# Moving an FFT convolution's spectral product from VectorE to GpSimd, and attention's weights-times-values product to split fp32r form

## The chip, the cores and the metric

The kernel runs on one core of a Trainium2 chip. The metric is the device time of one execution in microseconds. The kernel before takes 966.35 us, the median of three runs (965.32 to 966.81).

## What is computed

One layer of a bidirectional encoder on 512 tokens of width 1024, in float32: half a SwiGLU step, a mixing stage, another half SwiGLU step, a final norm. The change lies in the mixing stage, whose two groups of heads share one input projection:

```python
p = h @ w_in                                   # q | k | v | hyena x0 | x1 | v
logits = einsum('bqhcd,bkhcd->bhcqk', q, k) * scale + bias
attn   = softmax(logits)[c=0] - lam * softmax(logits)[c=1]     # 4 heads, two maps each
out    = einsum('bhqk,bkhe->bqhe', attn, v)                    # weights times values
...
v = v * x1                                     # hyena, after a width-3 convolution
y = irfft(rfft(v, n=2L) * rfft(kern, n=2L))[:L]                # long convolution
y = (y + v * filt_bias) * x0
```

## The kernel before, in words

Everything is laid out as 128 partitions by 512 tokens. TensorE (PE) does every large product in fp32r, a form that takes one pass but keeps fewer bits; so that nothing is lost, each operand x is held as x_hi, an fp32r copy made by ScalarE (ACT), and x_lo = x - x_hi, made by VectorE (DVE), and a product is three passes, hi·hi, hi·lo and lo·hi. A plain float32 product takes one instruction, which the trace records twice.

The mixing stage is a program written out by hand for each engine; semaphores keep the engines apart, and the order on each engine is fixed. PE runs 24 `project(n)` tiles (24 matmuls each: 8 blocks k by 3 passes), and between them the attention of head h = 0 to 3:

- `two_scores(h, qb)`: query times key for two query blocks, into banks 2 to 5. It waits for `qk_split` (DVE's `split_qk`, the low parts of q and k).
- DVE `logits(h, qb)` adds the bias (bank and bias, 128x512, twice); ACT `exps(h, qb)` takes exponentials and their sums; DVE `combine(h, qb)` forms one block of `attn` in three instructions: a reciprocal, a small `scalar_tensor_tensor` on two columns of `stat` (L1788), and a wide one on the two halves of `prob` (L1791).
- PE `attend_turns(h)` waits for all four blocks (`attn_set`) and transposes key blocks kt = 0 and 1 of `attn` into banks 4 and 5 (L2557, four transposes a block); ACT `attn_turns` copies each to `attn_t` (L1006). It stands behind k = 6 of `project(13)`, `project(17)` or `project(21)`.
- PE `attend(h)` multiplies `v_nat` by `attn_t` for four key blocks (L2576), in plain float32 for heads 0 to 2, with the turns of kt = 2 and 3 between the products, since there are two banks. Head 3 (`last_attend`) has the split form: `v_hi`, `v_lo`, `attn_hi` and `attn_low`.

DVE has more to do between these: `project(n)` reads a finished tile from its bank (times `rinv`), `split(8, n)` makes the low part of the next weights from `raw` and `w_hi` (L1227), `taps(n)` does two steps of the short convolution on `zpad` and `x0c` (L1746, L1747), and the spectral product of the long convolution is spread in pairs of instructions over heads 0 to 2: `cross_near`, `cross_far`, `own_near`, `own_far`, `imaginary`, `real`, `real_parities`, `imaginary_parities`, for the two halves f = 0 and 1 of the frequencies, 16 instructions each. The half f can begin when DVE's `cosines(f)` and `sines(f)` are done (`spec_read`). PE's `inverse(g)`, in head 3, waits for `spec_set` 2, the end of the last pair.

GpSimd (POOL) has in this stage only the four DMA issues of `bias`, one a head. Elsewhere it adds squares for the norms (L585) with a 128x512 `tensor_tensor`.

Of the kernel before, what the change touches and what calls it, by code (L numbers as in the profile page):

```python
# [14 lines left out]
P = 128  # L15
D = 1024
S = 512
# [86 lines left out]
def build(nc, a, out):  # L104
    ctx = ExitStack()
    with ctx:
# [74 lines left out]
        def h_high(ffn, f):  # L181
# [41 lines left out]
        v_nat, _ = place("v_nat", [P, NT, P], at=act3_at)  # L223
        v_hi, _ = place("v_hi", [P, NT, P], F32R, at=act3_at)
        v_lo, _ = place("v_lo", [P, NT, P], F32R, at=bias_at)
        attn_hi, _ = place("attn_hi", [P, NT, S], F32R, at=attn_t_at)
        attn_lows = [place(f"attn_lo{n}", [P, S], F32R, at=at + 4 * 3 * S)[0] for n, at in enumerate((x0c_at, vx_at))]
# [92 lines left out]
        dft_even, dft_sum, spec_even, evens_set, spec_read, spec_set, kern_evens = (  # L320
            sem(n) for n in ("dft_even", "dft_sum", "spec_even", "evens_set", "spec_read", "spec_set", "kern_evens"))
# [242 lines left out]
        def _(pool):  # L564
# [47 lines left out]
            for h in range(HEADS):  # L612
                wait(pool, logit_set, 2 * NT * (h - 1))
                toeplitz = bass.AP(vec_dram.tensor, vec_dram.offset + h * 2 * S, [[1, P], [1, bias_w]])
                pool.dma_start(bias[:, h % 2, :], toeplitz).then_inc(bias_landed[h % 2], 16)

# [12 lines left out]
        def _(act):  # L629
# [368 lines left out]
            def v_natural(h):  # L998
                act.wait_ge(v_turned, h + 1)
                nc.scalar.copy((v_hi if h == 3 else v_nat)[:], bank[TURN_BANKS[h]][:].rearrange("p (t c) -> p t c", t=NT)).then_inc(v_set, 1)  # L1000

            def attn_turns(h, kts):
                wait(act, att_col_sum, h)
                for kt in kts:
                    act.wait_ge(attn_turned, NT * h + kt + 1)
                    nc.scalar.copy((attn_hi if h == 3 else attn_t)[:, kt, :], bank[4 + kt % 2][:]).then_inc(attn_t_set, 1)  # L1006
# [100 lines left out]
            attn_turns(1, (0, 1))  # L1107
            split(8, N_MIX + 19)
            qk_high(2, 1)
            attn_turns(1, (2, 3))  # L1110
# [12 lines left out]
            attn_turns(2, (0, 1))  # L1123
            split(8, N_MIX + 23)
            qk_high(3, 1)
            attn_turns(2, (2, 3))
# [87 lines left out]
        def _(dve):  # L1214
# [542 lines left out]
            def v_low():  # L1757
                dve.wait_ge(v_set, HEADS)
                nc.vector.tensor_tensor(v_lo[:], bank[TURN_BANKS[3]][:].rearrange("p (t c) -> p t c", t=NT),
                                        v_hi[:].bitcast(F32), ALU.subtract).then_inc(v_split, 1)  # L1760

            def attn_low(kt):

                dve.wait_ge(attn_turned, NT * 3 + kt + 1)
                dve.wait_ge(attn_t_set, NT * 3 + kt + 1)
                nc.vector.tensor_tensor(attn_lows[kt % 2][:], bank[4 + kt % 2][:], attn_hi[:, kt, :].bitcast(F32),
                                        ALU.subtract).then_inc(attn_split, 1)
# [29 lines left out]
            def kernel_parities(c):  # L1797

                dve.wait_ge(kern_even, c + 1)
                even, twice = bank[4][:], ksig[:, 2 * c + 1, :]  # L1800
                nc.vector.tensor_tensor(ksig[:, 2 * c, :], even, twice, ALU.add)
                x, y = (twice, even) if c else (even, twice)
                nc.vector.tensor_tensor(twice, x, y, ALU.subtract).then_inc(kern_evens, 1)
                dve.wait_ge(kern_evens, c + 1)
# [13 lines left out]

            def mult(dst, x, y):
                return nc.vector.tensor_tensor(dst, x, y, ALU.mult)  # L1820

            t0, t1, t2, t3 = (prod[:, i, :] for i in range(4))
# [22 lines left out]
            def sines(f):  # L1845
# [6 lines left out]
                dve.wait_ge(spec_read, f + 1)  # L1852

            def cross_near(f):
                near_a, far_a, near_b, far_b = parts(f)
                dve.wait_ge(kern_set, 4)
                mult(t0, near_a, kern_q[:, f, :])
                link(mult(t1, near_b, kern_p[:, f, :]))

            def cross_far(f):  # L1860
                near_a, far_a, near_b, far_b = parts(f)
                mult(t2, far_a, kern_q[:, 2 + f, :])
                link(mult(t3, far_b, kern_p[:, 2 + f, :]))

            def own_near(f):
                near_a, far_a, near_b, far_b = parts(f)
                mult(near_a, near_a, kern_p[:, f, :])
                link(mult(near_b, near_b, kern_q[:, f, :]))

            def own_far(f):  # L1870
                near_a, far_a, near_b, far_b = parts(f)
                mult(far_a, far_a, kern_p[:, 2 + f, :])
                link(mult(far_b, far_b, kern_q[:, 2 + f, :]))

            def imaginary(f):

                nc.vector.tensor_tensor(t0, t0, t1, ALU.add)
                link(nc.vector.tensor_tensor(t2, t2, t3, ALU.add))

            def real(f):  # L1880

                near_a, far_a, near_b, far_b = parts(f)
                nc.vector.tensor_tensor(kern_p[:, f, :], near_a, near_b, ALU.subtract)
                link(nc.vector.tensor_tensor(kern_p[:, 2 + f, :], far_a, far_b, ALU.subtract))

            def real_parities(f):

                near, far = kern_p[:, f, :], kern_p[:, 2 + f, :]
                nc.vector.tensor_tensor(kern_q[:, f, :], near, far, ALU.add)
                link(nc.vector.tensor_tensor(kern_q[:, 2 + f, :], near, far, ALU.subtract))  # L1890

            def imaginary_parities(f):

                nc.vector.tensor_tensor(kern_p[:, f, :], t0, t2, ALU.subtract)
                nc.vector.tensor_tensor(kern_p[:, 2 + f, :], t0, t2, ALU.add).then_inc(spec_set, 1)
                dve.wait_ge(spec_set, f + 1)
# [106 lines left out]
            cross_near(0)  # L2003
# [12 lines left out]
            own_far(0)  # L2016
            combine(1, 0)
            logits(1, 1)
            imaginary(0)
            project(14)  # L2020
            combine(1, 1)
            real(0)
            split(8, N_MIX + 16)
            real_parities(0)
# [8 lines left out]
            imaginary_parities(0)  # L2033
            project(16)
            split(8, N_MIX + 18)
            cross_near(1)
            project(17)
            split_qk(2, 0)
            split_qk(2, 1)
            cross_far(1)  # L2040
# [3 lines left out]
            own_near(1)  # L2044
            combine(2, 0)
            logits(2, 1)
            own_far(1)
            project(18)
            combine(2, 1)
            imaginary(1)  # L2050
            split(8, N_MIX + 20)
            real(1)
# [8 lines left out]
            real_parities(1)  # L2061
            project(20)
            split(8, N_MIX + 22)
            imaginary_parities(1)
            project(21)
            split_qk(3, 0)
# [34 lines left out]
            v_low()  # L2101
            attn_low(0)
            attn_low(1)
            split(8, N_OUT + 1)
            attn_low(2)
            attn_low(3)
# [69 lines left out]
        def _(pe):  # L2176
# [294 lines left out]
            def two_scores(h, qb):  # L2471

                if qb == 0:
                    pe.wait_ge(logit_set, 2 * NT * h)
                    pe.wait_ge(attn_t_set, NT * h)
# [49 lines left out]
            def turn_v(h):  # L2525
# [3 lines left out]
                wait(pe, v_set, h)  # L2529
# [22 lines left out]
            def turn(h, kt):  # L2552
                if h == 3:
                    wait(pe, attn_split, kt - 1)
                wait(pe, attn_t_set, NT * h + kt - 1)
                for qb in range(NT):
                    ins = nc.tensor.transpose(bank[4 + kt % 2][:, qb * P:(qb + 1) * P],  # L2557
# [3 lines left out]
            def attend_turns(h):  # L2561
# [4 lines left out]
                turn(h, 0)  # L2566
                turn(h, 1)

            def attend(h):
# [9 lines left out]
                ins.then_inc(pv_sum, 1)  # L2579

            def last_attend():
                pe.wait_ge(att_o_set, 3)
                pe.wait_ge(v_split, 1)
                for kt in range(NT):
                    pe.wait_ge(attn_t_set, NT * 3 + kt + 1)
                    nc.tensor.matmul(bank[6][:], v_hi[:, kt, :], attn_hi[:, kt, :], start=kt == 0, stop=False)
                    nc.tensor.matmul(bank[6][:], v_lo[:, kt, :], attn_hi[:, kt, :], start=False, stop=False)
                    pe.wait_ge(attn_split, kt + 1)
                    ins = nc.tensor.matmul(bank[6][:], v_hi[:, kt, :], attn_lows[kt % 2][:], start=False, stop=kt == NT - 1)
                    if kt + 2 < NT:  # L2590
                        turn(3, kt + 2)
                ins.then_inc(pv_sum, 1)

            def att_sums(h):
# [4 lines left out]
                else:  # L2599
                    pe.wait_ge(v_set, 3)  # L2600
# [83 lines left out]
            def out_half(n, jj):  # L2684
# [3 lines left out]
                if part and jj == 0:  # L2688
                    if pair == 1:
                        pe.wait_ge(hy_scaled, NG)  # L2690
                    elif pair == 2:
                        pe.wait_ge(attn_split, NT)
# [75 lines left out]
            project(13, between={6: lambda: attend_turns(0)})  # L2768
# [9 lines left out]
            project(17, between={6: lambda: attend_turns(1)})  # L2778
# [9 lines left out]
            project(21, between={6: lambda: attend_turns(2)})  # L2788
# [16 lines left out]
            last_attend()  # L2805
# [116 lines left out]
```

## Time and profile before

| | |
|---|---|
| median of three runs | 966.35 us |
| the profiled execution, device time | 966.17 us |
| its span in the profile | 964.4 us |
| PE busy | 958.1 us (99%) |
| PE weight loads busy | 826.7 us (86%) |
| DVE busy | 693.2 us (72%) |
| ACT busy | 439.9 us (46%) |
| POOL busy | 87.9 us (9%) |

The span is what the profiler saw from the first to the last instruction; the device time has 1.8 us around it. Matmuls overlap in their pipeline, and the end that the profile shows for one is modelled: the pace of PE is read from start to start, not from durations. A start of a DVE instruction that waits for a port lies before the wait, so the wait shows as a longer instruction.

### The profile page before, as it was taken

How to read it: one execution, taken by the hardware profiler on the slowest of the kernel's cores; microseconds unless marked ns; L12 is line 12 of the kernel's file. 1: busy time of each engine (PE TensorE's matmuls, PEld its weight loads, DVE VectorE, ACT ScalarE, POOL GpSimd, SP SyncE). 2: the span in 40 equal slices, each digit the busy share in tenths (PEclk: the TensorE clock that was granted, in tenths of full speed). 3: DMA queues.
4: the chain of work that ended last, by engine and by line, in shares of the span. 5: the costliest groups of instructions: out<-in, count | busy, mean ns of one | idle time of the engine just before them, and what ended most of it. 6: DMA issues, size and time to landing. Idle time of an engine off the chain costs nothing.

```text
span 964.4 us, 15111 instructions
## 1 busy us (share of the span) xinstructions
PE 958.1 (99%) x5487; PEld 826.7 (86%) x5487; DVE 693.2 (72%) x1072; ACT 439.9 (46%) x699; POOL 87.9 (9%) x104
## 2 busy tenths in 40 slices
PE   9999999999999999999999999999999999999998
PEld 8889999999888887677777878889999999988887
DVE  6888897887754438868898775789897788742333
ACT  6345665546333233244455563446565554622222
POOL 0011121210011010000000000001112121000100
PEclk9999999999999999999999999999999999999999
DMA  7456768674433336121221332256777767333322
GB/s 228 142 142 174 197 169 196 169 192 141 138 99 101 99 125 240 66 81 51 84 86 45 113 117 88 92 149 155 187 193 171 203 162 191 102 104 99 90 69 88
DMA packets 55029, 128.67 MB, mean 133 GB/s; under 512 B 5954, under 2 KB 14287, under 8 KB 54724
## 3 DMA queue, kind: packets, MB, share of 16 engines
q1 hardware_dynamic: 44452, 107.31, 34.7%
q0 software_dynamic: 10384, 20.67, 12.3%
q8 instruction: 30, 0.49, 0.2%
q14 instruction: 19, 0.16, 0.1%
q10 hardware_dynamic: 144, 0.05, 0.1%
HBM read 123.78 MB, written 4.22 MB: 133 GB/s over the span
## 4 chain that ended last, share of the span: by engine, by line
PE 94%; DVE 3%; issue 1%; ACT 1%; DVEq 0%; POOL 0%; ACTq 0%; POOLq 0%
PE bank L2185 14%; PE bank L2187 14%; PE bank L2186 14%; PE bank L2243 8%; PE bank L2242 8%; PE bank L2241 8%; PE bank L2233 7%; PE bank L2235 3%; PE bank L2705 1%; PE bank L2707 1%; PE bank L2706 1%; PE bank L2576 1%; PE bank L2328 1%; PE bank L2329 1%; PE bank L2330 1%
## 5 line engine op out<-in xcount | busy, mean ns | idle before, releaser
L1227 DVE TENSOR_TENSOR w_lo<-raw,w_hi 128x1024 fp32r<-128x1024 f32 (+1 forms) x94 | 113.2, 1204 | 105.9 <-ACT w_hi L638 105.6
L638 ACT CAST w_hi<-raw 128x1024 fp32r<-128x1024 f32 (+1 forms) x94 | 95.0, 1011 | 187.4 <-PE bank L2187 172.4
L2185 PE MATMUL bank<-x_hi,w_hi 128*128 128x512 f32 x320 | 128.3, 401 | 0.1
L2186 PE MATMUL bank<-h_lo,w_hi 128*128 128x512 f32 x330 | 128.4, 389 | 0.0
L2187 PE MATMUL bank<-x_hi,w_lo 128*128 128x512 f32 x320 | 124.7, 390 | 0.0
L2186 PE MATMUL bank<-x_lo,w_hi 128*128 128x512 f32 x320 | 124.7, 390 | 0.0
L2241 PE MATMUL bank<-xt_both,w_hi 128*128 128x256 f32 x408 | 115.6, 283 | 0.0
L2243 PE MATMUL bank<-xt_both,w_lo 128*128 128x256 f32 x408 | 115.5, 283 | 0.0
L2242 PE MATMUL bank<-xt_both,w_hi 128*128 128x256 f32 x408 | 115.4, 283 | 0.0
L2241 PEld LDWEIGHTS bank<-xt_both,w_hi 128*128 128x128 f32 x408 | 77.6, 190 | 0.1
L2243 PEld LDWEIGHTS bank<-xt_both,w_lo 128*128 128x128 f32 x408 | 77.6, 190 | 0.0
L2242 PEld LDWEIGHTS bank<-xt_both,w_hi 128*128 128x128 f32 x408 | 77.6, 190 | 0.0
L2242 PE MATMUL bank<-xt_both,wt_hi 128*128 128x256 f32 x272 | 77.0, 283 | 0.0
L2243 PE MATMUL bank<-xt_both,wt_lo 128*128 128x256 f32 x272 | 77.0, 283 | 0.0
L2241 PE MATMUL bank<-xt_both,wt_hi 128*128 128x256 f32 x272 | 76.7, 282 | 0.0
L2185 PEld LDWEIGHTS bank<-x_hi,w_hi 128*128 128x128 f32 x320 | 60.1, 188 | 17.2 <-issue 5.6
L2186 PEld LDWEIGHTS bank<-h_lo,w_hi 128*128 128x128 f32 x330 | 61.9, 188 | 12.8
L2187 PEld LDWEIGHTS bank<-x_hi,w_lo 128*128 128x128 f32 x320 | 60.1, 188 | 12.8
L2186 PEld LDWEIGHTS bank<-x_lo,w_hi 128*128 128x128 f32 x320 | 60.2, 188 | 12.3 <-issue 0.7
L2185 PE MATMUL bank<-h_hi_t,w_hi 128*128 128x512 f32 x180 | 70.0, 389 | 0.0
L2187 PE MATMUL bank<-h_hi_t,w_lo 128*128 128x512 f32 x180 | 70.0, 389 | 0.0
L1494 DVE TENSOR_TENSOR wt_lo<-raw,wt_hi 128x1024 fp32r<-128x1024 f32 x34 | 41.6, 1224 | 29.7 <-ACT wt_hi L758 29.5
(392 smaller groups left out, 2142.6 us busy)
## 6 DMA issues: line engine op xcount, KB each, us to landing
raw<-in_ffn_w_down SPq DMA_DIRECT2D x32, 512.0 KB, 3.6
raw<-in_ffn_w_gate SPq DMA_DIRECT2D x25, 512.0 KB, 4.0
raw<-in_ffn_w_up SPq DMA_DIRECT2D x25, 512.0 KB, 4.6
raw<-in_w_in SPq DMA_DIRECT2D x24, 512.0 KB, 3.3
raw<-in_ffn_w_gate SPq DMA_DIRECT2D x34, 256.0 KB, 3.1
raw<-in_ffn_w_up SPq DMA_DIRECT2D x34, 256.0 KB, 3.1
raw<-in_ffn_w_down SPq DMA_DIRECT2D x16, 384.0 KB, 3.1
sums<-in_ffn_w_gate SPq DMA_DIRECT2D x17, 256.0 KB, 3.7
```

The lines of the kernel that those rows point to most:

```text
L638: nc.scalar.copy(w_hi[:, half, 0:kb, :], raw[:, slot, 0:kb, :]).then_inc(w_hi_made, 1)
L1227: nc.vector.tensor_tensor(w_lo[:, half, 0:kb, :], raw[:, slot, 0:kb, :], w_hi[:, half, 0:kb, :].bitcast(F32), ALU.subtract).then_inc(w_spl ...
L1494: nc.vector.tensor_tensor(wt_lo[:, 0:2].rearrange("p t k c -> p (t k) c"), raw[:, 2 * b, :, :], hi.bitcast(F32), ALU.subtract).then_inc(pa ...
L2185: nc.tensor.matmul(dst, w_hi[:, half, k, :], hi, start=first and k == 0, stop=False)
L2186: nc.tensor.matmul(dst, w_hi[:, half, k, :], lo, start=False, stop=False)
L2187: ins = nc.tensor.matmul(dst, w_lo[:, half, k, :], hi, start=False, stop=last and k == kb - 1)
L2233: nc.tensor.matmul(bank[n][:], high[:, k, :], xt_both[ffn][:, m, k].rearrange("p t c -> p (t c)"), start=start and k == 0, stop=False, ski ...
L2235: ins = nc.tensor.matmul(second_half(n), low[:, k, :], xt_hi[ffn][:, m, k, :], start=False, stop=k == 3, skip_group_check=True)
L2241: nc.tensor.matmul(dst, high[:, k, :], xt_hi[ffn][:, m, k, :], start=start and k == 0, stop=False, skip_group_check=True)
L2242: nc.tensor.matmul(dst, high[:, k, :], xt_lo[ffn][:, m, k, :], start=False, stop=False, skip_group_check=True)
L2243: ins = nc.tensor.matmul(dst, low[:, k, :], xt_hi[ffn][:, m, k, :], start=False, stop=which == 3 and k == 3, skip_group_check=True)
L2328: nc.tensor.matmul(dst, hi[:, k, :], h_ops[1][f][0][:, tokens], start=f == 0, stop=False)
```

## The change

The spectral product leaves DVE. POOL does it in `spectrum(f)`, pair by pair, with a wait for its own semaphore behind each pair; the bias transfers of heads 2 and 3 are issued behind `spectrum(0)` and `spectrum(1)`. Attention's product takes the split form in all heads: `v_low` and `attn_low` on DVE for each head, three passes on PE for each key block. For heads 0 to 2 all four key blocks are turned at once, into banks 4, 5, 2 and 3, behind k = 5 of the project tile instead of k = 6. ACT copies the four blocks in a row; `qk_high(h+1, 1)` moves ahead of a weight split.

```diff
+            def two(dsts, xs, ys, ops):
+                made[0] += 1
+                nc.gpsimd.tensor_tensor(dsts[0], xs[0], ys[0], ops[0])
+                nc.gpsimd.tensor_tensor(dsts[1], xs[1], ys[1], ops[1]).then_inc(spec_made, 1)
+                pool.wait_ge(spec_made, made[0])
+
+            def spectrum(f):
+                near_a, near_b, far_a, far_b = ((sig0, sig1)[f][:, i, :] for i in range(4))
+                t0, t1, t2, t3 = (prod[:, i, :] for i in range(4))
+                p_near, p_far, q_near, q_far = (kern[:, i, :] for kern in (kern_p, kern_q) for i in (f, 2 + f))
+                pool.wait_ge(kern_set, 4)
+                pool.wait_ge(spec_read, f + 1)
+                two((t0, t1), (near_a, near_b), (q_near, p_near), (ALU.mult, ALU.mult))
+                two((t2, t3), (far_a, far_b), (q_far, p_far), (ALU.mult, ALU.mult))
+                two((near_a, near_b), (near_a, near_b), (p_near, q_near), (ALU.mult, ALU.mult))
+                two((far_a, far_b), (far_a, far_b), (p_far, q_far), (ALU.mult, ALU.mult))
+                two((t0, t2), (t0, t2), (t1, t3), (ALU.add, ALU.add))
+                two((p_near, p_far), (near_a, far_a), (near_b, far_b), (ALU.subtract, ALU.subtract))
+                two((q_near, q_far), (p_near, p_near), (p_far, p_far), (ALU.add, ALU.subtract))
+                nc.gpsimd.tensor_tensor(p_near, t0, t2, ALU.subtract)
+                nc.gpsimd.tensor_tensor(p_far, t0, t2, ALU.add).then_inc(spec_set, 1)
+                pool.wait_ge(spec_set, f + 1)
+
+            head_bias(0)
+            head_bias(1)
+            spectrum(0)
+            head_bias(2)
+            spectrum(1)
+            head_bias(3)
...
             qk_high(1, 0)
-            attn_turns(0, (0, 1))
+            attn_turns(0, range(NT))
+            qk_high(1, 1)
             split(8, N_MIX + 15)
-            qk_high(1, 1)
-            attn_turns(0, (2, 3))
             attended(0)
...
             combine(0, 2)
-            cross_near(0)
             logits(0, 3)
             project(12)
             combine(0, 3)
-            cross_far(0)
+            v_low(0)
             split(8, N_MIX + 14)
+            split_qk(1, 0)
+            attn_low(0, 0)
+            attn_low(0, 1)
+            attn_low(0, 2)
             project(13)
-            split_qk(1, 0)
+            attn_low(0, 3)
             split_qk(1, 1)
-            own_near(0)
             split(8, N_MIX + 15)
 
             logits(1, 0)
-            own_far(0)
             combine(1, 0)
...
-                turn(h, 0)
-                turn(h, 1)
+                for kt in range(2 if h == 3 else NT):
+                    turn(h, kt)
 
             def attend(h):
                 wait(pe, att_o_set, h)
                 if h in (1, 2):
                     pe.wait_ge(att_mean, h)
-                pe.wait_ge(v_set, h + 1)
+                pe.wait_ge(v_split, h + 1)
                 for kt in range(NT):
                     pe.wait_ge(attn_t_set, NT * h + kt + 1)
-                    ins = nc.tensor.matmul(bank[6][:], v_nat[:, kt, :], attn_t[:, kt, :], start=kt == 0, stop=kt == NT - 1)
-                    if kt + 2 < NT:
+                    nc.tensor.matmul(bank[6][:], v_hi[:, kt, :], attn_hi[:, kt, :], start=kt == 0, stop=False)
+                    nc.tensor.matmul(bank[6][:], v_low_part(h)[:, kt, :], attn_hi[:, kt, :], start=False, stop=False)
+                    pe.wait_ge(attn_split, NT * h + kt + 1)
+                    ins = nc.tensor.matmul(bank[6][:], v_hi[:, kt, :], attn_low_part(h, kt)[:], start=False, stop=kt == NT - 1)
+                    if h == 3 and kt + 2 < NT:
                         turn(h, kt + 2)
...
-            project(13, between={6: lambda: attend_turns(0)})
+            project(13, between={5: lambda: attend_turns(0)})
```

DVE's order changes in heads 1 and 2 as in head 0. `two_scores(h+1, 0)` waits for `attn_split` instead of `attn_t_set`, since DVE now reads the turned banks too. The low parts lie in parts of `vx` and `x0c` that are free by then.

## Rows read from the trace of the kernel before

**Rows 1.** The page: TensorE's granted clock by slice, and the chain that ended last.
```profile
PEclk9999999999999999999999999999999999999999
...
PE 94%; DVE 3%; issue 1%; ACT 1%; DVEq 0%; POOL 0%; ACTq 0%; POOLq 0%
```

**Rows 2.** PE's timeline, head 2: start, length, instruction, how many in a row.
```profile
502.08 0.39 PE L2185 MATMUL bank<-x_hi,w_hi 128*128 128x512 f32 x1
...
507.98 0.39 PE L2187 MATMUL bank<-x_hi,w_lo 128*128 128x512 f32 x1
508.30 0.50 PE L2486 MATMUL bank<-k_hi,q_hi 64*128 64x512 f32 x2
...
525.88 1.02 PE L2576 MATMUL bank<-attn_t,v_nat 128*128 128x512 f32 x2
526.73 0.60 PE L2557 MATMUL bank<-ident,attn 128*128 128x128 f32 x4
527.17 1.02 PE L2576 MATMUL bank<-attn_t,v_nat 128*128 128x512 f32 x2
528.03 0.60 PE L2557 MATMUL bank<-ident,attn 128*128 128x128 f32 x4
528.74 1.98 PE L2576 MATMUL bank<-attn_t,v_nat 128*128 128x512 f32 x4
530.65 0.50 PE L2486 MATMUL bank<-k_hi,q_hi 64*128 64x512 f32 x2
```

**Rows 3.** PE's timeline, head 0: block k = 6, the turns, the first product, the next scores.
```profile
459.22 0.39 PE L2185 MATMUL bank<-x_hi,w_hi 128*128 128x512 f32 x1
...
459.90 1.03 PE L2557 MATMUL bank<-ident,attn 128*128 128x128 f32 x8
...
461.47 1.02 PE L2576 MATMUL bank<-attn_t,v_nat 128*128 128x512 f32 x2
...
465.96 0.51 PE L2486 MATMUL bank<-k_hi,q_hi 64*128 64x512 f32 x2
```

**Rows 4.** The groups of instructions: copies of turned blocks, and low parts from a bank.
```profile
L1006 ACT COPY attn_t<-bank 128x512 f32<-128x512 f32 x12 | 6.7, 585 | 1.9 <-PE bank L2557 1.9
L1766 DVE TENSOR_TENSOR attn_lo<-bank,attn_hi 128x512 fp32r<-128x512 f32 x4 | 2.7, 685 | 1.0 <-ACT attn_hi L1006 1.0
```

**Rows 5.** One line, POOL's 128x512 additions: shortest, median and longest in ns.
```profile
L585 POOL TENSOR_TENSOR ssq<-ssq,sq x15: 1287/1294/1717, 255.6 to 941.8; 128x512 f32<-128x512 f32 x15
```

**Rows 6.** Timelines of POOL and DVE where an addition on POOL meets a DVE instruction.
```profile
342.28 1.30 POOL L585 TENSOR_TENSOR ssq<-ssq,sq 128x512 f32<-128x512 f32 x1 [13.67 <-ACT sq L646]
...
342.70 1.43 DVE L1282 SCALAR_TENSOR_TENSOR x_lo<-resid,cols,x_hi 128x512 fp32r<-128x512 f32 x1 [1.31 <-ACT x_hi L651]
...
357.13 0.75 DVE L1282 SCALAR_TENSOR_TENSOR x_lo<-resid,cols,x_hi 128x512 fp32r<-128x512 f32 x1 [0.79 <-ACT x_hi L651]
358.07 1.23 DVE L1227 TENSOR_TENSOR w_lo<-raw,w_hi 128x1024 fp32r<-128x1024 f32 x1 [0.19 <-ACT w_hi L638]
...
358.73 1.72 POOL L585 TENSOR_TENSOR ssq<-ssq,sq 128x512 f32<-128x512 f32 x1 [15.15 <-ACT sq L646]
...
911.78 1.29 POOL L585 TENSOR_TENSOR ssq<-ssq,sq 128x512 f32<-128x512 f32 x1 [13.68 <-ACT sq L646]
...
912.59 1.56 DVE L1227 TENSOR_TENSOR w_lo<-raw,w_hi 128x1024 fp32r<-128x1024 f32 x1 [1.11 <-ACT w_hi L638]
```

**Rows 7.** DVE's timeline from the first half's sines to head 0's last combine.
```profile
441.77 0.68 DVE L1851 TENSOR_TENSOR sig<-sig,bank 128x512 f32<-128x512 f32 x1
...
447.48 0.22 DVE L1788 SCALAR_TENSOR_TENSOR stat<-stat,lam 128x1 f32<-128x1 f32 x1
...
453.38 0.75 DVE L1791 SCALAR_TENSOR_TENSOR attn<-prob,stat 128x512 f32<-128x512 f32 x1
...
458.11 0.75 DVE L1791 SCALAR_TENSOR_TENSOR attn<-prob,stat 128x512 f32<-128x512 f32 x1
```

**Rows 8.** PE's timeline: the first matmul of the inverse transform, in head 3.
```profile
537.82 0.60 PE L2639 MATMUL bank<-sin_i,kern_p 128*128 128x128 f32 x4
```

More of the change, by code:

```diff
@@ L222, in build, with v_low_part, attn_low_part, turned_bank @@
         assert top[0] <= tail_end
[L223 removed]
         v_hi, _ = place("v_hi", [P, NT, P], F32R, at=act3_at)
[L225 removed]
+        v_lows = [place(f"v_lo{n}", [P, NT, P], F32R, at=at)[0] for n, at in enumerate((vx_at + 4 * S, bias_at))]
         attn_hi, _ = place("attn_hi", [P, NT, S], F32R, at=attn_t_at)
[L227 removed]
+        attn_lows = [place(f"attn_lo{n}", [P, S], F32R, at=at)[0]
+                     for n, at in enumerate((vx_at, vx_at + 4 * 3 * S, vx_at + 4 * 2 * S, x0c_at + 4 * 3 * S))]
+        def v_low_part(h):
+            return v_lows[h == 3]
+        def attn_low_part(h, kt):
+            return attn_lows[kt] if h < 3 else attn_lows[1 if kt % 2 else 3]
+        def turned_bank(h, kt):
+            return bank[4 + kt % 2] if h == 3 or kt < 2 else bank[kt]
         q_lo, _ = place("q_lo", [P, S], F32R, at=q_t_at)
@@ L611, in _, with head_bias @@
             nc.gpsimd.memset(zpad[:], 0.0).then_inc(consts_set, 1)
-            for h in range(HEADS):
+            def head_bias(h):
                 wait(pool, logit_set, 2 * NT * (h - 1))
@@ L999, in v_natural @@
                 act.wait_ge(v_turned, h + 1)
-                nc.scalar.copy((v_hi if h == 3 else v_nat)[:], bank[TURN_BANKS[h]][:].rearrange("p (t c) -> p t c", t=NT)).then_inc(v_set, 1)
+                nc.scalar.copy(v_hi[:], bank[TURN_BANKS[h]][:].rearrange("p (t c) -> p t c", t=NT)).then_inc(v_set, 1)
             def attn_turns(h, kts):
@@ L1005, in attn_turns @@
                     act.wait_ge(attn_turned, NT * h + kt + 1)
-                    nc.scalar.copy((attn_hi if h == 3 else attn_t)[:, kt, :], bank[4 + kt % 2][:]).then_inc(attn_t_set, 1)
+                    nc.scalar.copy(attn_hi[:, kt, :], turned_bank(h, kt)[:]).then_inc(attn_t_set, 1)
             def attended(h):
@@ L1106, in _ @@
             qk_high(2, 0)
-            attn_turns(1, (0, 1))
+            attn_turns(1, range(NT))
+            qk_high(2, 1)
             split(8, N_MIX + 19)
-            qk_high(2, 1)
-            attn_turns(1, (2, 3))
             attended(1)
@@ L1122, in _ @@
             qk_high(3, 0)
-            attn_turns(2, (0, 1))
+            attn_turns(2, range(NT))
+            qk_high(3, 1)
             split(8, N_MIX + 23)
-            qk_high(3, 1)
-            attn_turns(2, (2, 3))
             attended(2)
@@ L1755, in taps, with v_low, attn_low @@
                     nc.vector.tensor_tensor(far, count(1 + S, -1), count(1, 1), ALU.subtract).then_inc(vx_set, 1)
-            def v_low():
-                dve.wait_ge(v_set, HEADS)
-                nc.vector.tensor_tensor(v_lo[:], bank[TURN_BANKS[3]][:].rearrange("p (t c) -> p t c", t=NT),
+            def v_low(h):
+                dve.wait_ge(v_set, h + 1)
+                nc.vector.tensor_tensor(v_low_part(h)[:], bank[TURN_BANKS[h]][:].rearrange("p (t c) -> p t c", t=NT),
                                         v_hi[:].bitcast(F32), ALU.subtract).then_inc(v_split, 1)
[L1762 to L1766, printed above, removed]
+            def attn_low(h, kt):
+                dve.wait_ge(attn_turned, NT * h + kt + 1)
+                dve.wait_ge(attn_t_set, NT * h + kt + 1)
+                nc.vector.tensor_tensor(attn_low_part(h, kt)[:], turned_bank(h, kt)[:], attn_hi[:, kt, :].bitcast(F32),
                                         ALU.subtract).then_inc(attn_split, 1)
@@ L1802, in kernel_parities @@
                 x, y = (twice, even) if c else (even, twice)
-                nc.vector.tensor_tensor(twice, x, y, ALU.subtract).then_inc(kern_evens, 1)
-                dve.wait_ge(kern_evens, c + 1)
+                link(nc.vector.tensor_tensor(twice, x, y, ALU.subtract))
             def kernel_spectrum(k):
@@ L1851, in sines @@
                 nc.vector.tensor_tensor(near_b, near_b, sin_odd, ALU.add).then_inc(spec_read, 1)
[L1852 to L1896, printed above, removed]
             def long_read_out(g):
@@ L2032, in _ @@
             att_means(0)
-            imaginary_parities(0)
+            v_low(1)
             project(16)
             split(8, N_MIX + 18)
-            cross_near(1)
+            split_qk(2, 0)
+            attn_low(1, 0)
+            attn_low(1, 1)
+            attn_low(1, 2)
             project(17)
-            split_qk(2, 0)
+            attn_low(1, 3)
             split_qk(2, 1)
-            cross_far(1)
             split(8, N_MIX + 19)
             logits(2, 0)
-            own_near(1)
             combine(2, 0)
             logits(2, 1)
-            own_far(1)
             project(18)
             combine(2, 1)
-            imaginary(1)
             split(8, N_MIX + 20)
-            real(1)
             logits(2, 2)
@@ L2060, in _ @@
             att_means(1)
-            real_parities(1)
+            v_low(2)
             project(20)
             split(8, N_MIX + 22)
-            imaginary_parities(1)
+            split_qk(3, 0)
+            attn_low(2, 0)
+            attn_low(2, 1)
+            attn_low(2, 2)
             project(21)
-            split_qk(3, 0)
+            attn_low(2, 3)
             split_qk(3, 1)
@@ L2100, in _ @@
             hy_low(3)
-            v_low()
-            attn_low(0)
-            attn_low(1)
+            v_low(3)
+            attn_low(3, 0)
+            attn_low(3, 1)
             split(8, N_OUT + 1)
-            attn_low(2)
-            attn_low(3)
+            attn_low(3, 2)
+            attn_low(3, 3)
             split(8, N_OUT + 2)
@@ L2474, in two_scores @@
                     pe.wait_ge(logit_set, 2 * NT * h)
-                    pe.wait_ge(attn_t_set, NT * h)
+                    wait(pe, attn_split, NT * h)
                 for q in (qb, qb + 1):
@@ L2528, in turn_v @@
                 pe.wait_ge(spec_read, 2)
-                wait(pe, v_set, h)
+                wait(pe, v_split, h)
                 if h == 3:
@@ L2552, in turn @@
             def turn(h, kt):
-                if h == 3:
-                    wait(pe, attn_split, kt - 1)
-                wait(pe, attn_t_set, NT * h + kt - 1)
+                wait(pe, attn_split, NT * h + (kt - 1 if h == 3 else 0))
                 for qb in range(NT):
-                    ins = nc.tensor.transpose(bank[4 + kt % 2][:, qb * P:(qb + 1) * P],
+                    ins = nc.tensor.transpose(turned_bank(h, kt)[:, qb * P:(qb + 1) * P],
                                               attn[:, qb, kt * P:(kt + 1) * P], ident[:])
@@ L2599, in att_sums @@
                 else:
-                    pe.wait_ge(v_set, 3)
+                    pe.wait_ge(v_split, 3)
                 if h == 2:
@@ L2691, in out_half @@
                     elif pair == 2:
-                        pe.wait_ge(attn_split, NT)
+                        pe.wait_ge(attn_split, NT * HEADS)
                     elif pair == 3:
@@ L2777, in _ @@
             project(16)
-            project(17, between={6: lambda: attend_turns(1)})
+            project(17, between={5: lambda: attend_turns(1)})
             attend(1)
@@ L2787, in _ @@
             project(20)
-            project(21, between={6: lambda: attend_turns(2)})
+            project(21, between={5: lambda: attend_turns(2)})
             attend(2)
@@ L2804, in _ @@
             first_out({0: lambda: spread(3)})
-            last_attend()
+            attend(3)
             out_tile(1)
```

23 lines of the change are left out of this document (3 added, 20 removed).

## The prediction

> **What bounds the kernel now.** I began with the page: the chain that ended last is 94% PE, and the granted clock is full, 2.4 GHz, in every slice [rows 1]. So time is what PE's stream contains, plus any moment at which it waits. The profiled execution took 966.17 us (span 964.4, 1.77 around it); the median is 966.35, so the sum below may start from either. Next I read PE's timeline where the change is, start to start [rows 2, 3], then DVE's just ahead of head 0's turns [rows 7], because DVE sets when PE may turn, and last the few places where POOL computes beside DVE [rows 5, 6].
>
> **PE's own saving.** An fp32r pass takes (507.98 - 502.08)/26 = 0.227 us; the step from such a pass into the scores is 0.32, 0.1 more [rows 2]. A plain product takes 0.85 (525.88 to 526.73), four transposes 0.44 (526.73 to 527.17), and there is a wait of 528.74 - 528.03 - 0.44 = 0.27 for ACT's copy [rows 2]. Head 2's attend lasts 525.88 to 530.65, 4.77, of which 0.88 is turns: 3.89. Head 1 repeats it within 0.02. Head 0's is 4.49 (461.47 to 465.96), 3.61 without turns [rows 3]. The new one is 12 passes of 0.227 and the step of 0.1, 2.82. Saved: 0.79 + 1.08 + 1.07 = 2.94 us. The turns only move: sixteen transposes a head, as before, so nothing. If no new wait comes, that is 966.17 - 2.94 = 963.2.
>
> **What the new product waits for.** After four turns (1.75) come k = 6 and 7 (1.36), then the first pass, 3.1 us behind the first turn. Four copies of 0.585 on ACT and four `attn_low` of 0.685 on DVE [rows 4], the latter back to back, keep up with 0.68 us a key block if DVE is there when the first copy is, about 1.2 us behind the first turn. Ahead of them DVE has `v_low` (0.6), a weight split (1.2) and `split_qk` (0.6): 2.4. So DVE must end `combine(h, 3)` some two us ahead of the time at which PE would like to turn. The semaphore changes (`v_split` for `v_set`, `attn_split` for `attn_t_set`) cost nothing: the last pass of `attend` has already waited for them.
>
> **DVE's relief.** 32 spectral instructions go, 15 low parts come, each about 0.6 at its pace. In head 0 two of them stood ahead of `logits(0, 3)`, so its last combine, over at 458.86 [rows 7], would be over near 457.5. PE reaches the turns, now ahead of k = 6, at 459.22 [rows 3]: 1.7 us of slack.
>
> **POOL's price.** A 128x512 addition takes 1.29 us on POOL [rows 5]; multiply and subtract have no row and are taken as the same, with zero to 2.6 each as bounds. 32 of them are 41 us. POOL starts when the first sines are done, 441.77 + 0.69 = 442.5 [rows 7], and fills heads 0 and 1. Its own deadline is far: even stretched by half it ends near 505, and `inverse` starts at 537.82 [rows 8]. The bias of head 2 goes out near 469, a head (32 us, half of 465.96 to 530.65) ahead of its use. Alone, POOL costs nothing.
>
> But it isn't alone. When `x_lo` began at 342.70, inside POOL's addition of 342.28 to 343.58, it took 1.43 instead of 0.75, ending 0.55 behind the addition; `w_lo` at 912.59, inside 911.78 to 913.07, took 1.56 instead of 1.23; and the addition that began at 358.73 inside `w_lo` took 1.72 instead of 1.29 [rows 6]. All eleven meetings in the trace look so: whoever is second stands still until the first is done. In each the DVE instruction reads two operands from SBUF. The Trainium skill (SBUF — State Buffer, Who interferes with whom) makes it a rule: the two engines share a port pair, locked for a whole instruction, and a VectorE instruction with at most one SBUF input doesn't take it. By that rule logits, bank reads and low parts stay free; no row shows one under an addition. I count them as free, the nearest rows having two SBUF inputs; if they too are held, head 0 gains eight more meetings of up to 1.29 each.
>
> **Head 0, worked through.** Between 442.5 and the last combine DVE has nine instructions with two SBUF inputs: three combines of two (L1788, L1791), a split, two taps. I let additions run back to back (0.1 between pairs), let a waiting DVE instruction in when one ends, and give it 0.55 from there (1.1 for a split). `combine(0, 1)`: the small one waits from 447.48 to addition 4's end, 447.8; the wide one comes behind addition 5 and ends 449.75. The split waits for addition 7 and ends 453.6. The taps end 455.45 and 457.3, behind 8 and 9. `combine(0, 2)` waits for 10 and for 11 and ends 460.6 (before 454.13 [rows 7]). Logits, a read and ACT's exponentials take until 463.0; the last combine, behind additions 13 and 14, ends at 465.3. PE wanted it at 459.2: a wait of **6.1 us**. What follows is late with it: `split(14)` and `split_qk` meet additions 15 and 16, the low parts end about 1.4 later than the passes want them, and `split_qk(1, 1)` holds the next scores 1.5 more. In head 1 PE runs ten us of tiles before it asks, DVE nearly catches up while `spectrum(1)` runs to about 497, and I get 0.8. Head 2 has no POOL work: zero. Sum: 6.1 + 1.4 + 1.5 + 0.8 - 2.94 = +6.9.
>
> Bounds: from below, the small instruction (one column; no row) isn't held and close races go to DVE; the last combine ends at 461 to 462, PE waits 2 to 3, the rest 1: about 0. From above, DVE lets both additions of a pair pass each time: nine more of 1.29. I take **+6**, near the schedule and a little to the low side: **972.2**, rounded to 972, likely 968.3 to 976.
>
> **Rivals.** *The saving comes through (other side).* The mechanism: DVE's waits are absorbed by its slack, because POOL gives way within an instruction, or DVE's idle time covers it. For it: DVE is relieved of 17 instructions net, and PE's stream is shorter by rows that are sure. Against: all eleven meetings. It decides the sign if head 0's combine ends within 2.9 us of 459.2; with no wait at all 963.2. Chance 0.27.
>
> *It cancels.* The lower bound above: contention is real, but waits and saving balance, 964.4 to 968.3. Chance 0.13.
>
> *PE's clock falls behind the wait.* In this trace PE is never left for 6 us and is always at full clock [rows 1], so no row shows what a long gap does. If it dropped to 1.2 GHz for k = 6, 7 and one attend, 18 passes would take twice 0.227: 4 us more, 976. Its point of decision is a wait as long as mine or longer. The Trainium skill (TensorE: Matmul & The Clock Gate, Part 1) says that an idle engine falls to the lower of its two clocks; no run here shows it yet. Chance 0.15.
>
> *The change doesn't do what it says.* POOL late at `inverse` would need 2.9 us an instruction, over twice the row; under 0.02, left out.
>
> **How the numbers follow.** Slower, my forecast, 0.45; with a lower clock 0.15; cancelling 0.13; faster 0.27. A measurement of this kernel tells about 0.2%, 1.9 us, from no change. So faster 0.27, same 0.13, slower 0.60. The range holds most of the faster case and part of the clock's: 962.8 to 977. Without the faster case, 967 to 977.
>
> **What the profile of the changed kernel would show.** PE: `attend` as 12 starts 0.227 apart (if 0.3, the saving is gone). POOL: 32 instructions from 442.5; lengths beyond 1.29 wherever DVE holds it. DVE: L1788 and L1791 of heads 0 and 1 longer by up to 1.3, back at 0.22 and 0.75 in head 2; logits unchanged if one SBUF input is free. PE waits ahead of head 0's first turn, for DVE's `attn`. If L1791 keeps 0.75 beside running POOL additions, my forecast is wrong at its root; if it is held but PE doesn't wait, I misjudged the slack; if the granted clock leaves 1.0 there, the third rival adds to it.

## The result, and the profile after

The changed kernel takes 972.42 us (median of six runs, 972.0 to 972.91) against 966.36 us for the kernel before on the same chip: ratio 1.0064, 95% interval 1.0055 to 1.0074. It is slower by 6.06 us; 972 was predicted. The profiled execution took 972.0 us, its span is 970.2.

PE's timeline of the changed kernel, head 0 and the first events of the later heads (start, length, instruction, count, and in brackets idle time and what ended it); it answers to [rows 2, 3]:

```profile
458.66 0.39 PE L2177 MATMUL bank<-x_hi,w_lo 128*128 128x512 f32 x1
465.18 3.45 PE L2545 MATMUL bank<-ident,attn 128*128 128x128 f32 x16 [6.13 <-DVE attn L1833]
468.39 0.47 PE L2175 MATMUL bank<-x_hi,w_hi 128*128 128x512 f32 x1
...
469.86 0.40 PE L2564 MATMUL bank<-attn_hi,v_hi 128*128 128x512 f32 x1
470.09 0.39 PE L2565 MATMUL bank<-attn_hi,v_lo 128*128 128x512 f32 x1
470.32 0.40 PE L2567 MATMUL bank<-attn_lo,v_hi 128*128 128x512 f32 x1
...
473.33 0.50 PE L2476 MATMUL bank<-k_hi,q_hi 64*128 64x512 f32 x2 [0.57 <-DVE k_lo L1761]
...
498.66 1.91 PE L2545 MATMUL bank<-ident,attn 128*128 128x128 f32 x16
...
504.60 0.50 PE L2476 MATMUL bank<-k_hi,q_hi 64*128 64x512 f32 x2
...
535.85 0.50 PE L2476 MATMUL bank<-k_hi,q_hi 64*128 64x512 f32 x2
```

The new product is there as written: passes 0.23 us apart. Ahead of head 0's turns PE stands still for 6.13 us, for the last block of `attn`. Those 16 turns then take 468.39 - 465.18 = 3.21 us; in head 1, without a wait ahead, the same 16 go to the next block in 1.67. The windows of the changed kernel say why (length, busy time and count of PE, weight loads, DVE, ACT and POOL, granted clock, DMA share, GB/s):

```profile
458.60:465.20 6.60, 0.47 (x3) 0.08 (x2) 6.16 (x11) 2.98 (x6) 6.44 (x6) 0.72 0.00 0
465.20:468.40 3.20, 3.20 (x17) 3.20 (x17) 3.20 (x3) 1.56 (x3) 2.88 (x4) 0.52 0.24 74
468.40:472.60 4.20, 4.20 (x21) 3.27 (x18) 4.11 (x7) 2.03 (x4) 4.12 (x3) 1.00 0.54 178
```

Behind the wait the granted clock is 0.52, close to the lower of the two levels (1.2 GHz), for some 3.2 us; then it is full again. The kernel before was at full clock throughout [rows 1].

DVE's timeline of the changed kernel, same stretch as [rows 7], shows where the 6 us come from:

```profile
446.91 0.54 DVE L1830 SCALAR_TENSOR_TENSOR stat<-stat,lam 128x1 f32<-128x1 f32 x1
447.49 1.87 DVE L1833 SCALAR_TENSOR_TENSOR attn<-prob,stat 128x512 f32<-128x512 f32 x1
...
451.11 1.87 DVE L1269 TENSOR_TENSOR w_lo<-raw,w_hi 128x1024 fp32r<-128x1024 f32 x1
452.90 1.78 DVE L1788 SCALAR_TENSOR_TENSOR x0c<-zpad,cols,x0c 128x512 f32<-128x512 f32 x1
454.71 1.67 DVE L1789 SCALAR_TENSOR_TENSOR x0c<-zpad,cols,x0c 128x512 f32<-128x512 f32 x1
...
456.61 0.94 DVE L1830 SCALAR_TENSOR_TENSOR stat<-stat,lam 128x1 f32<-128x1 f32 x1
457.58 1.86 DVE L1833 SCALAR_TENSOR_TENSOR attn<-prob,stat 128x512 f32<-128x512 f32 x1
459.37 0.68 DVE L1821 CUSTOM_DVE_ANT_0 logit<-bank,bias 128x512 f32<-128x512 f32 x1
...
461.84 1.32 DVE L1830 SCALAR_TENSOR_TENSOR stat<-stat,lam 128x1 f32<-128x1 f32 x1
463.20 1.84 DVE L1833 SCALAR_TENSOR_TENSOR attn<-prob,stat 128x512 f32<-128x512 f32 x1
...
472.02 1.26 DVE L1761 TENSOR_TENSOR k_lo<-k_t,k_hi 128x512 fp32r<-128x512 f32 x1
```

Every instruction with two SBUF inputs here is longer: the wide combine takes 1.84 to 1.87 us (0.75 in head 2), a split 1.87 instead of 1.23 [rows 6], and the one-column instruction of `combine` 0.54 to 1.32. The logits, with one input from a bank, keep 0.68. POOL's timeline of the changed kernel is the other half of it:

```profile
442.27 1.29 POOL L633 TENSOR_TENSOR prod<-sig,kern_q 128x512 f32<-128x512 f32 x1 [79.80 <-DVE sig L1887]
...
448.78 1.74 POOL L634 TENSOR_TENSOR sig<-sig,kern_q 128x512 f32<-128x512 f32 x1
...
451.85 2.28 POOL L634 TENSOR_TENSOR sig<-sig,kern_q 128x512 f32<-128x512 f32 x1
...
490.11 1.31 POOL L652 TENSOR_TENSOR kern_p<-prod 128x512 f32<-128x512 f32 x1
```

A multiplication takes 1.29 us like the additions of [rows 5], up to 2.28 where DVE got in first, and all 32 are over at 491.4.

How far PE is behind the kernel before, by starts in the two traces, each difference worked out here:

| PE's event | before | after | difference |
|---|---|---|---|
| ready for head 0's turns | 459.22 (k = 6) | 458.89 | -0.33 |
| first turn of head 0 in the new order | | 465.18 | |
| scores of head 1 | 465.96 | 473.33 | +7.37 |
| scores of head 2 | 498.32 | 504.60 | +6.28 |
| scores of head 3 | 530.65 | 535.85 | +5.20 |
| inverse transform | 537.82 | 543.02 | +5.20 |

(458.89 is the last pass's start and 0.23.) So head 0 loses 7.7 us, heads 1 and 2 give back 1.09 and 1.08, and 5.2 stay to the end of the stage. The spans differ by 5.8, the medians by 6.06.

### The profile page after: what moved, and what is told of

It is laid out like the page before. It is cut to its first block, busy times and chain, and to the rows that moved or that the text cites. A ratio compares the mean times of both kernels' runs of the same rounds, so it can differ in the third digit from the quotient of the medians.

```text
span 970.2 us, 15148 instructions
## 1 busy us (share of the span) xinstructions
PE 956.4 (99%) x5499; PEld 829.7 (86%) x5499; DVE 697.2 (72%) x1055; ACT 439.8 (45%) x699; POOL 134.7 (14%) x136
## 4 chain that ended last, share of the span: by engine, by line
PE 95%; DVE 3%; issue 1%; ACT 1%; DMA 0%; DVEq 0%; SPq 0%; ACTq 0%
PE bank L2175 15%; PE bank L2177 15%; PE bank L2176 15%; PE bank L2233 8%; PE bank L2232 8%; PE bank L2231 8%; PE bank L2223 7%; PE bank L2225 3%; PE bank L2683 1%; PE bank L2685 1%; PE bank L2684 1%; PE bank L2545 1%; PE bank L2318 1%; PE bank L2319 1%; PE bank L2320 1%
## 5 line engine op out<-in xcount | busy, mean ns | idle before, releaser
L1269 DVE TENSOR_TENSOR w_lo<-raw,w_hi 128x1024 fp32r<-128x1024 f32 (+1 forms) x94 | 116.4, 1239 | 106.1 <-ACT w_hi L683 105.9
```

The costliest lines, as they stand in the source:

```text
L1269: nc.vector.tensor_tensor(w_lo[:, half, 0:kb, :], raw[:, slot, 0:kb, :], w_hi[:, half, 0:kb, :].bitcast(F32), ALU.subtract).then_inc(w_spl ...
```

## The experiments

Unless said otherwise an edit is against the changed kernel, and a time is a median beside that of the kernel before on the same chip. The edits are shown abridged, with comments added.

**GpSimd without reads.** POOL's 32 arithmetic instructions become writes of zeros of nearly the same length, into places nobody reads; the spectral product is left out.

```
-nc.gpsimd.tensor_tensor(dsts[0], xs[0], ys[0], ops[0])
+nc.gpsimd.memset(scratch[0], 0.0)      # 1440 columns
```

> The changed kernel with each of GpSimd's 32 arithmetic instructions replaced by a memset of 1440 columns, about as long (1.3 us by the memset of 1560 columns at 1.39), at the same places and with the same waits; the spectral product is left out, nothing else. Theory (GpSimd's reads lock out VectorE's instructions with two SBUF operands): the wide combine keeps 0.75 us, PE does not wait ahead of head 0's turns, and the saving of 2.9 us shows: 963 to 964 us. Rival A (any GpSimd activity holds VectorE): 971 to 973 us. Rival B (the wait of 6 us comes from the turns' earlier place and VectorE's new order, not from GpSimd): 971 to 973 us.

963.31 us against 966.31, ratio 0.997 (0.9959 to 0.9981). In its trace (POOL, DVE's wide combine as a group with shortest, median and longest ns, and PE):

```profile
442.46 1.30 POOL L633 MEMSET prod<- 128x1440 f32 x1 [79.73 <-DVE sig L1888]
```
```profile
L1834 DVE SCALAR_TENSOR_TENSOR attn<-prob,stat x16: 750/752/753, 437.3 to 551.7; 128x512 f32<-128x512 f32 x16
```
```profile
459.11 1.91 PE L2546 MATMUL bank<-ident,attn 128*128 128x128 f32 x16
...
465.06 0.50 PE L2477 MATMUL bank<-k_hi,q_hi 64*128 64x512 f32 x2
```

POOL runs through all of head 0 as in the changed kernel (its last write ends at 484.8 us), and no wide combine is longer than 0.753. PE's saving is all there: 3.0 us. So POOL's running alone does not hold DVE; its arithmetic, which reads SBUF, does. And neither the new product nor the earlier place of the turns, which are both in this run, costs anything.

**The spectral product on GpSimd alone.** The kernel before with only that part of the change; its attention product stays plain float32. It stands in two forms: the first kept one semaphore more and has no time; the second has an existing link on DVE in its place. The expectations are in that order.

```
-            cross_near(0)        # and the 15 other pairs, on DVE
+            spectrum(0)          # on POOL, then spectrum(1)
-  nc.vector.tensor_tensor(twice, x, y, ALU.subtract).then_inc(kern_evens, 1)
-  dve.wait_ge(kern_evens, c + 1)
+  link(nc.vector.tensor_tensor(twice, x, y, ALU.subtract))
```

> The kernel before with the spectral product on GpSimd as in the changed kernel, and nothing else of the change. Theory: head 0's last combine is as late as in the changed kernel, about 465 us, PE waits some 5.6 us from the turns' later place, its clock falls for about 1.5 us, no saving comes back: 973 to 975 us. Rival B (split form and turns): about 965 to 966 us.

> The kernel before with the spectral product on GpSimd as in the changed kernel, and nothing else of the change (the kernel of e3 with one semaphore less). Theory: head 0's last combine is as late as in the changed kernel, about 465 us, PE waits some 5.6 us from the turns' later place, its clock falls for about 1.5 us, no saving comes back: 973 to 975 us. Rival (the wait needs the split form and the turns' earlier place): about 965 to 966 us.

973.49 us against 966.24, ratio 1.0075 (1.0059 to 1.009). PE's timeline, and two windows behind its wait:

```profile
465.13 1.94 PE L2575 MATMUL bank<-ident,attn 128*128 128x128 f32 x8 [5.46 <-DVE attn L1826]
...
474.09 0.51 PE L2504 MATMUL bank<-k_hi,q_hi 64*128 64x512 f32 x2
```
```profile
465.20:468.40 3.20, 3.20 (x12) 2.91 (x13) 2.00 (x2) 1.18 (x2) 2.88 (x4) 0.50 0.26 72
468.40:470.80 2.40, 2.40 (x7) 1.25 (x7) 2.40 (x3) 1.57 (x2) 2.32 (x2) 0.50 0.90 273
```

The time is as expected. The loss comes with this half: `attn` is ready at the same moment as in the full change (first turns at 465.13 and 465.18), and the clock falls as well. Here the low clock lasts to 470.8 and costs more than the 1.5 us expected: from the first turn to the next scores this run takes 8.96 us (465.13 to 474.09), the kernel before 6.06 (459.90 to 465.96), so 2.9 us.

**The split product alone.** The spectral product goes back to DVE; since four low parts now stand between the last combine and `split_qk`, the pairs that stood there move behind `split_qk`.

```
-            spectrum(0)          # POOL, and spectrum(1)
             split_qk(1, 1)
+            cross_far(0)         # DVE, and so on
+            own_near(0)
```

> The changed kernel with the spectral product on VectorE again, in the places of the kernel before as far as they are not between a head's last combine and its split_qk (those go behind split_qk). Theory: no lock, saving of 2.9 us less some waits, as VectorE now has both loads (28 of 32 us a head plus 3): 963.3 to 965.5 us. Rival (VectorE cannot carry both, which would be the reason for GpSimd): 967 us or more.

966.8 us against 966.31, ratio 1.0008 (0.9998 to 1.0017): the expectation is missed. Its waits of PE from head 2's first scores to the inverse transform (engine, line, what it waits for, us in total, times, longest):

```profile
PE bank L2652 <- issue: 1.1, 1, 1.1
PE bank L2210 <- DVE w_lo L1238: 0.6, 1, 0.6
PE bank L2511 <- DVE k_lo L1730: 0.3, 1, 0.3
```

The scores start at 464.92, 496.23 and 529.08: heads 0 and 1 have the saving, head 1 at 31.31 us; head 2 takes 32.85, and the inverse transform stands 1.1 us more. It starts at 537.55 behind `logits(3, 1)`, which DVE ends at 537.44. There 0.27 us of the saving is left (the kernel before starts it at 537.82). DVE cannot carry the pairs and the new low parts both in this order, and the saving goes into that. Whether another order on DVE could carry both was not tried.

**GpSimd's instructions in other places.** First version: two pairs at once, seven pairs behind head 1's `split_qk` and seven behind head 2's, to spare head 0.

```
+if n == 2: pool.wait_ge(qk_split, 4)
+if n == 9: pool.wait_ge(qk_split, 6)
```

> The changed kernel with GpSimd's 16 pairs held back: two pairs at once, seven from the end of head 0's work (qk_split 4), seven from the end of head 1's (qk_split 6); same arithmetic. Theory (what costs is the lock in the 16 us ahead of head 0's last combine, where VectorE has under 2 us of slack): head 0 runs free, heads 1 and 2 take 14 instructions each as head 1 of the changed kernel took 12 without a wait of PE: 963 to 964.5 us, faster than both kernels. Rival B (turns' place and VectorE's order): 971 to 973 us. Rival C (the total of the lock counts, wherever it falls): 968 us or more.

966.23 us, ratio 1.0005 (0.9996 to 1.0014); missed too. Head 0 has no wait any more (turns at 459.02, scores at 464.97), but head 1 takes 33.04 us and head 2 32.11, where 31.25 is free of waits. PE's waits in it:

```profile
PE bank L2181 <- DVE w_lo L1275: 0.8, 1, 0.8
PE bank L2482 <- DVE k_lo L1767: 0.6, 2, 0.3
```

The list has 1.4 of the 2.65 us lost; the rest stands between starts of PE, where the modelled ends hide it. Fourteen instructions in a row were too many for DVE's slack in head 1 and in head 2 alike, while the changed kernel's head 1 (31.27 us) took about twelve without a wait of PE. Second version: one or two at a time, each behind a semaphore after which DVE is about to read banks or to wait.

```
+some(4)                                   # all waits are of POOL
+pool.wait_ge(attn_set, 2); some(1); pool.wait_ge(attn_set, 3); some(2)
+pool.wait_ge(qk_split, 3); some(2)
+for h in (1, 2):                          # at = N_MIX + 16 + 4 * (h - 1)
+    w_split at: 2, attn_set 4h+1: 2, w_split at+1: 2, w_split at+2: 1,
+    attn_set 4h+4: 1, qk_split 2h+3: 2
+# 3 more in head 3; inverse waits for spec_made 32
```

> The changed kernel with GpSimd's 32 instructions let go one or two at a time where VectorE has instructions with one SBUF operand or waits for ScalarE: four at once, then behind attn_set 2 and 3, behind split_qk, and in heads 1 and 2 ten each (logits, reads of tiles, low parts), the last three in head 3. Theory (the lock costs only where it meets a two-operand instruction on a tight chain): VectorE's combines and splits keep nearly their own lengths, PE waits under 1 us in all: 963.2 to 964.5 us, faster than both kernels and than e2. Rival (the total of GpSimd's reads counts, or one-operand instructions are held too): 966 us or more.

963.23 us against 966.24, ratio 0.9972 (0.996 to 0.9983): faster than both kernels. Its groups, one place in POOL's and DVE's timelines, and the window of heads 1 and 2:

```profile
L660 POOL TENSOR_TENSOR prod<-sig,kern_q x4: 1291/1293/1302, 442.4 to 493.3; 128x512 f32<-128x512 f32 x4
L1856 DVE SCALAR_TENSOR_TENSOR attn<-prob,stat x16: 750/752/753, 437.2 to 551.6; 128x512 f32<-128x512 f32 x16
```
```profile
466.00 1.28 POOL L660 TENSOR_TENSOR prod<-prod 128x512 f32<-128x512 f32 x1 [2.07 <-DVE w_lo L1292]
```
```profile
466.06 0.69 DVE L1844 CUSTOM_DVE_ANT_0 logit<-bank,bias 128x512 f32<-128x512 f32 x1 [0.15 <-PE bank L2501]
```
```profile
470.00:530.00 60.00, 60.00 (x311) 48.39 (x310) 46.49 (x93) 30.45 (x58) 24.87 (x21) 1.00 0.19 61
```

The same 32 instructions read the same tiles, but mostly beside bank reads: all of POOL's take 1.28 to 1.30 us, and the wide combines keep their length. A few short instructions of DVE with two SBUF inputs are still held (`combine`'s small one takes 0.78 and 0.44 us in head 0 instead of 0.22), where nobody waits for them: PE waits for nothing from 455 to 540.

**PE kept busy through the wait.** 26 matmuls into a bank that is free there, ahead of head 0's wait.

```
+if h == 0:
+    for _ in range(26):
+        nc.tensor.matmul(bank[6][:], w_hi[:, 1, 0, :], x_hi[:, 0, :], start=True, stop=True)
 pe.wait_ge(attn_set, NT * (h + 1))
```

> The changed kernel with 26 more matmuls (5.9 us, into bank 6, which head 0's product overwrites) ahead of the wait for head 0's last combine. The result is the same. Theory: PE's granted clock stays at 1.0, the 16 turns take 1.7 us instead of 3.2; head 0's low parts then come late by about 0.7 us, as they are no longer hidden by the slow turns, so 0.5 to 1.5 us come back: 970.9 to 971.9 us. Rival (the turns are slow for another reason than the idle stretch): 972.4 us or more.

971.55 us, ratio 1.0055 (1.0041 to 1.0069). PE's and DVE's timelines, and the window that read 0.52:

```profile
458.99 6.06 PE L2555 MATMUL bank<-x_hi,w_hi 128*128 128x512 f32 x26
464.89 1.91 PE L2545 MATMUL bank<-ident,attn 128*128 128x128 f32 x16
...
472.66 0.51 PE L2476 MATMUL bank<-k_hi,q_hi 64*128 64x512 f32 x2 [1.31 <-DVE k_lo L1761]
...
535.94 0.50 PE L2476 MATMUL bank<-k_hi,q_hi 64*128 64x512 f32 x2
```
```profile
461.94 0.22 DVE L1830 SCALAR_TENSOR_TENSOR stat<-stat,lam 128x1 f32<-128x1 f32 x1
462.20 1.68 DVE L1833 SCALAR_TENSOR_TENSOR attn<-prob,stat 128x512 f32<-128x512 f32 x1
...
470.89 1.72 DVE L1761 TENSOR_TENSOR k_lo<-k_t,k_hi 128x512 fp32r<-128x512 f32 x1
```
```profile
465.20:468.40 3.20, 3.20 (x23) 2.75 (x21) 3.20 (x4) 2.06 (x4) 2.88 (x3) 1.00 0.40 127
```

The clock stays at 1.00 and the turns are back at 1.66 us, 1.55 less: the idle stretch had brought the slow clock. Little of that arrives. Some passes of `attn_lo` now stand 0.1 to 0.2 us each, the wait for `k_lo` is 1.31 instead of 0.57, and the next scores are 0.67 us earlier (472.66 against 473.33). That much is DVE's: in both kernels these scores start as `k_lo` ends (472.61 and 473.28). DVE is earlier because a race went the other way. Its one-column instruction got ahead of POOL's 14th (0.22 us instead of 1.32), and the last combine ended at 463.88 instead of 465.04; the filler held PE until 464.89.

Head 1 loses the 0.67 us again: the scores of head 2 start at 504.65 (504.60 in the changed kernel), those of head 3 at 535.94 (535.85), PE's last instruction at 964.18 (964.13). So the time is as expected, 5.31 us over the reference against 6.06, but the traces don't show where those 0.75 us come from, and not that the clock gives them. DVE is late in either case; a PE at half clock had hidden it.

**The small instruction with one SBUF operand.** The 128x1 instruction of `combine` keeps its arithmetic, with one tensor and two scalars.

```
-scalar_tensor_tensor(stat[:, 3:4], s0, lam[:, 5:6], stat[:, 2:3], ALU.mult, ALU.mult)
+tensor_scalar(stat[:, 3:4], stat[:, 2:3], s0, lam[:, 5:6], ALU.mult, ALU.mult)
```

> The changed kernel with the small instruction of combine (one column, two SBUF operands and a scalar) written as a tensor_scalar with one operand and two scalars; same arithmetic. Theory (a second SBUF operand is what takes the shared port, however short the instruction is): the small one keeps its length beside GpSimd (in the changed kernel head 0's three grew to 0.54, 0.94 and 1.32 us), and head 0's last combine ends 1 to 2 us earlier: 970 to 971.5 us. Rival (the wide one behind it only waits longer for the same addition): 972 to 973 us.

972.12 us, ratio 1.0062 (1.0048 to 1.0076): no gain that can be measured, and the expectation is missed. In DVE's and PE's timelines, and two windows behind PE's waits:

```profile
458.90 0.27 DVE L1830 TENSOR_SCALAR stat<-stat,lam 128x1 f32<-128x1 f32 x1
```
```profile
460.95 3.40 PE L2545 MATMUL bank<-ident,attn 128*128 128x128 f32 x16 [1.98 <-DVE attn L1833]
...
471.11 0.51 PE L2476 MATMUL bank<-k_hi,q_hi 64*128 64x512 f32 x2 [2.43 <-DVE k_lo L1761]
```
```profile
461.00:464.00 3.00, 3.00 (x16) 3.00 (x17) 3.00 (x3) 1.64 (x3) 3.00 (x2) 0.54 0.00 0
...
471.10:474.30 3.20, 3.19 (x14) 2.17 (x15) 3.20 (x4) 0.38 (x1) 3.20 (x2) 0.56 0.06 8
```

Scalars are not held: 0.27 us. The turns come 4.2 us earlier, but now the wait for `k_lo` is 2.43, the clock falls twice, and by the scores of head 3 (535.65 against 535.85) 0.2 us is left. The time lies in the rival's range, though not by the rival's mechanism. A meeting avoided in one place is a meeting in the next while POOL runs on: here `k_lo` takes 3.28 us.

## Why the prediction was right

**The saving** was right: heads 1 and 2 give 1.09 and 1.08 us (1.08 and 1.07 predicted), and where nothing else interferes the kernel takes 963.3 (writes of zeros) and 963.2 (slots), where 963.2 was worked out.

**The mechanism** was right: DVE instructions with two SBUF inputs are held by POOL's reading instructions, those with one or none are not. The trace agrees with the rule cited from the Trainium skill (SBUF — State Buffer, Who interferes with whom), which the page limits to instructions outside VectorE's 2-port modes (one input read through both ports): the logits keep 0.68 us beside POOL's running instructions. The schedule worked through put head 0's combines at 449.75, 460.6 and 465.3; they ended at 449.36, 459.44 and 465.04. The wait of 6.1 us measured 6.13 in the profile (6.29 start to start).

That it came out so close is partly luck. DVE reached the last combine 1.2 us earlier than in the schedule, and there it met POOL's 14th and 15th instructions, not the 13th and 14th. In the run with filler, where DVE and POOL have the same orders, the race for the 14th went the other way by less than 0.1 us (461.94 against 462.03), and the last combine ended 1.16 us earlier.

Two readings of the rows were off, without harm. The trace before has fourteen meetings, not eleven; all look alike. And the two us by which DVE should be ahead of the turns don't follow from the terms, 2.4 of work with 1.2 to spare; in the run with slots 1.16 us were enough (457.86 against 459.02).

**Three smaller terms were mis-sized.** The low parts were to cost 1.4 us and cost nothing: the slow turns gave DVE that time. `split_qk(1, 1)` was to cost 1.5 and cost 0.57. With PE at full clock both appear: the run with filler takes 4.64 us from the first pass to the scores, where 2.82 are free, so 1.8 together. Head 1 was to lose 0.8; it has no wait at all (31.27 us, and 31.28 in the run with slots). In their place came 1.54 us of slow turns, 3.21 less 1.67.

**The clock** was wrongly kept as a rival of its own: it came along with the likeliest case, and each of the four waits of 1.98 to 6.13 us shown above brought it. It was priced at 4 us, for 18 passes at half clock. With the spectral product alone on GpSimd, where PE was last, it cost 2.9 us. In the changed kernel it lasted about 3.2 us, and the passes of the product were already at full pace. It made the turns 1.54 us longer, but DVE stood in no wait from 463.2 to the end of `k_lo` at 473.28, and the scores had to wait for that in any case. So no net price of the clock is shown here: with filler, PE is no earlier from the scores of head 2 on.

The trace agrees with the Trainium skill's statement that an idle engine falls to the lower clock (TensorE: Matmul & The Clock Gate, Part 1): 0.52 of full clock behind the wait, 1.00 with work in its place.

**The sum.** Head 0 goes from 459.22 - 465.96, 6.74 us, to 458.89 - 473.33, 14.44: +6.29 for the wait, +1.45 for the turns (3.21 against two times 0.88), +0.10 for k = 6 and 7 (1.47 against 1.37) and -0.14 for the attend (3.47 against 3.61: its saving of 0.79 is mostly eaten by the 0.57 for `k_lo`), in all +7.70. With -1.09 and -1.08 from heads 1 and 2, and PE's arrival 0.33 us earlier, that is the +5.20 at head 3. Against the 6.9 worked out and the 6 taken, 6.06 is close partly because errors cancel; that 6 was taken and not 6.9 had no row behind it. Two differences stay open, and no run was made for either: the 0.33 us come from ahead of 360 us, and some 0.5 us of the span lies behind the end of the chain that ended last (4.0 us there, 3.5 in the kernel before).

## What to carry to other kernels

Price an instruction that is moved to GpSimd by the VectorE instructions with two SBUF inputs that it will meet, and by the slack of each of them, not by GpSimd's own time: the same 32 instructions gave +6.06 us in a row and -3.0 us in slots beside bank reads, both with the split product's saving of 2.94 in it. Work through VectorE's order by hand with each meeting in it; the late instruction that TensorE asks for first is most of the price. A wait hides the ones behind it and can bring a slower clock, so taking one away shows the next: move the whole source, not a single meeting.

## What the runs showed of the hardware

- The granted clock falls after short waits too: 0.52 behind 6.13 us, 0.50 behind 5.46, 0.54 behind 1.98, 0.56 behind 2.43; behind 1.31 us, in the run with filler, it stayed at 1.00 (472.60 to 475.80).
- The slow clock cost 2.9 us where PE was last (plain products); in the changed kernel DVE was, and the traces show no loss by it.
- One column with two SBUF inputs is held for the rest of a 128x512 instruction on GpSimd: 0.22 us (head 2) becomes 1.32.
- GpSimd's writes of zeros, 1.30 us each, hold no combine back: the wide instruction takes 0.750 to 0.753 in all 16.
- The hold works both ways: behind a weight split a GpSimd multiplication lasts 2.28 instead of 1.29 us.
